# Converting the up and down weights two chunks per transfer, with rows of 8 KB read and 4 KB written, on eight cores of a Trainium2

## The chip, the cores and the metric

The kernel runs on all 8 cores of one Trainium2 chip, one program for all of them. The metric is the device time of the slowest core in microseconds; a run is a median over executions. An integer input called `side` picks one of two instruction streams ("arms"): even cores run arm 0 (the first 2304 frames of a stream), odd cores run arm 1 (the remaining 1792 frames, preceded by a light pass over the first 2304 frames to get the recurrent state).

## The reference

One layer of a hybrid encoder, in float32, for 4 prompt streams of 4096 frames and 32 sample streams of 64 frames, D_MODEL = 1024:

```
h = RMSNorm(x);  [gB | gC | xA | xL | gL] = h @ w_in          # 1024 x 2560
outA = gB * conv3_causal(gC * xA)                             # 512 channels
outB = RG_LRU(conv4_causal(xL) + b) * gelu(gL)                # 512 channels, linear recurrence
x = x + concat([outA, outB]) @ w_out                          # 1024 x 1024
x = x + relu(RMSNorm(x) @ w_up)^2 @ w_down                    # 1024 x 4096, 4096 x 1024
y = RMSNorm(x)
```

The convolution and recurrence states are returned too.

## The kernel before

**Tiles of frames.** Arm 0 has five prompt tiles M0 to M4 of 512, 512, 512, 384 and 384 frames and one sample tile S of 256. Arm 1 has five light tiles L, the tile S and four M tiles. All matmuls are bf16 with float32 sums in PSUM.

**Weights.** w_in, w_up and w_down are cut into 84 chunks of 128 x 1024 numbers: chunks 0 to 19 are w_in, 20 to 51 (from `CH_UP`) w_up, 52 to 83 (from `CH_DOWN`) w_down. They arrive in float32 in `wall`, whose rows are 1024 numbers (4 KB) at a distance of 1040. A DMA issued from GpSimd's queue (queue 0, "software_dynamic") reads float32 and writes bf16, so a row becomes 2 KB. The w_in chunks are converted into SBUF (buffers `ring` and `uT`), used there by tiles S and M0, and copied back to the scratch `wscr` in HBM by SyncE's queue (queue 1). The w_up and w_down chunks are converted from HBM to HBM, `wscr<-wall`: 64 transfers, each 128 rows of 4 KB read and 2 KB written. `wout` goes to SBUF in four conversions whose rows are 8 KB read and 4 KB written.

**The ring.** Each time TensorE needs a chunk, SyncE loads it from `wscr` into one of the ring slots (256 KB, queue 1, 8 rows of 2 KB on each of the 16 DMA engines). Four slots exist until M0's projections are done, then eight; after M0's MLP eight more in `uS`. A load waits for the chunk's conversion (`scr_b[chunk]`) and for TensorE to have left the slot. Inputs x come on ScalarE's queue (queue 10).

**The order of the work.** A planner in Python (`Weaver`) simulates all strands with fixed costs and emits each engine's instructions in the order of the planned start times; on the chip the order is fixed and only semaphores decide times. `g_conv` is the strand of the conversions. Its constants:

```
PACE = {"cv": 6}                 # a conversion is planned no earlier than the landing of the sixth before it
W.CV = 4.4 if chunk < CH_UP else 6.5 if chunk < CH_DOWN else 7.5      # planned us per MB written
MARGIN = 20.0                    # planned us from a conversion's landing to the first load of it
```

and the last number of each DMA request is its size in MB (0.52 for a chunk). The planned landing of a conversion is the previous one's plus size times `CV`. GpSimd's stream holds, in order, these DMA issues, half of the squares of relu (line 535) and small copies; a square that waits holds up the conversions behind it. On the chip a conversion also waits for its semaphore, of which the pool `cv` has 24.

**Lines.** L112 issues all DMAs, L776 and L780 are the input projection (from first-use buffers and from the ring), L989 the output projection, L1037 w_up, L1087 w_down, L697 transposes, L535, L543, L532 helpers of VectorE and ScalarE.

Of the kernel before, what the change touches and what calls it, by code (L numbers as in the profile page):

```python
# [6 lines left out]
F32, BF16 = mybir.dt.float32, mybir.dt.bfloat16  # L7
# [7 lines left out]
CH_UP, CH_DOWN, NCHUNK = 20, 52, 84  # L15
# [3 lines left out]
WPAD = 1040  # L19
# [354 lines left out]
def build_program():  # L374
    nc = bass.Bass("TRN2", target_bir_lowering=False)

    def din(name, shape, dt=F32):
        return nc.dram_tensor(name, list(shape), dt, kind="ExternalInput").ap()

    def dout(name, shape, dt=F32):  # L380
        return nc.dram_tensor(name, list(shape), dt, kind="ExternalOutput").ap()

    xp, xl, xs = din("xp", [NF, D]), din("xl", [128, 8 * NF]), din("xs", [256, D])
    side_d = din("side", [1, 1], mybir.dt.int32)
    wall = din("wall", [NCHUNK, 128, WPAD])
    wout_d = din("wout", [128, 8 * 1024])
    par_d = din("par", [128, PAR_COLS])
    wbd_d = din("wbd", [128, 8 * 128])
    gf_d = din("gf", [D])
    yp, ys = dout("yp", [NF, D]), dout("ys", [256, D])  # L390
    stp_d, sts_d = dout("stp", [128, 24]), dout("sts", [128, 96])
    wscr = nc.dram_tensor("wscr", [NCHUNK, 128, 1024], BF16).ap()

    es = ExitStack()
    tensors, sems = {}, {}
# [11 lines left out]
    def arm(second_half):  # L407
        S = Sched(nc, es, sems)
# [4 lines left out]
        def sb(name, shape, dt=F32):  # L413
            return sbuf(name, shape, dt)

        ring = sb("ring", [128, R * 1024], BF16)
        ring_b = [Buf("ring%d" % i) for i in range(R)]
        slots = [(ring[:, i * 1024:(i + 1) * 1024], ring_b[i]) for i in range(R - 4)]
        wout = sb("wout", [128, 8 * 1024], BF16)
# [74 lines left out]
        ps = psum()  # L494
        bank_b = [Buf("bank%d" % i) for i in range(8)]
        scr_b = [Buf("scr%d" % i) for i in range(NCHUNK)]
        out_events = []

        P_x, P_hb, P_hT, P_T, P_A = Slots(range(8)), Slots(range(2)), Slots(range(NHT)), Slots(range(NT)), Slots(range(1))
        P_x.strict = True  # L500
        P_rs = Slots(range(2))
        P_bank, P_rl, P_stat = Slots(range(8)), Slots(range(3)), Slots(range(5))

        def bank_ap(b, n=512):
            return ps[:, b * 512:b * 512 + n]
# [16 lines left out]
        def PER(dur, mk, rd_, wr_, chunk):  # L522
            def load():
                ap, buf = slots.pop(0)
                slots.append((ap, buf))
                S.dma("sp", ap, wscr[chunk], [scr_b[chunk]], [buf], "ring")
                return ap, buf
            return ("op", "pe", dur, mk, rd_, wr_,
                    {"peek": lambda: (slots[0][1], None), "scr": scr_b[chunk], "load": load})
# [23 lines left out]
        def DMA(q, out, in_, rd_, wr_, pool, mb, **kw):  # L553
            return ("dma", q, out, in_, rd_, wr_, pool, mb, kw)
# [10 lines left out]
        def g_back(oc):  # L565
            ap, bufs = first[oc]
            yield tok(("used", oc))
            yield DMA("sp", wscr[oc], ap, bufs, [scr_b[oc]], "wb", 0.26)

        def g_conv(order):  # L570
            for chunk in order:
                W.CV = 4.4 if chunk < CH_UP else 6.5 if chunk < CH_DOWN else 7.5
                if chunk < CH_UP:
                    ap, bufs = first[chunk]
                    yield DMA("pool", ap, wall[chunk, :, 0:1024], [], bufs, "cv", 0.52)
                    W.spawn(g_back(chunk), 400)
                else:
                    yield DMA("pool", wscr[chunk], wall[chunk, :, 0:1024], [], [scr_b[chunk]], "cv", 0.52)
                if chunk == 15:
                    yield DMA("pool", wbd[:], wbd_d, [], [wbd_b], "par", 0.5)  # L580
                if chunk == 3:
                    for hf in range(4):
                        yield DMA("pool", wout[:, hf * 2048:(hf + 1) * 2048], wout_d[:, hf * 2048:(hf + 1) * 2048], [],
                                  [wout_b[hf]], "cv", 1.05)

        def g_setup():
            yield MSET("pool", identb[:], 0.0, [ident_b])
            yield OP("pool", 0.3, lambda e: e.affine_select(out=identb[:], in_=identb[:], compare_op=ALU.not_equal, fill=1.0,
                                                            base=0, pattern=[[-1, 128]], channel_multiplier=1), [ident_b], [ident_b])
            yield MSET("pool", onesf, 1.0, [ones_b])  # L590
            yield MSET("pool", cst[:, 0:1], 1.0, [cst_b])
            yield MSET("pool", cst[:, 1:2], EPS, [cst_b])
            for t_, bl in ((halx, halx_b), (halp, halp_b), (h0_p, h0_b)):
                yield MSET("pool", t_[:], 0.0, bl)
            W.mark("set0")
# [568 lines left out]
            yield DMA("sp", dst, so[:], [sob], [], "sto", 0.02, allow_slow_non_contiguous=True)  # L1164
            out_events.append(S.last_dma)

        order = [12, 13, 14, 15] + [16, 8, 4, 0, 17, 9, 5, 1, 18, 10, 6, 2, 19, 11, 7, 3] + list(range(CH_UP, NCHUNK))
        W.spawn(g_setup(), -20)
        W.spawn(g_conv(order), 500)
        W.spawn(g_par(), -19)  # L1170
        W.spawn(g_xloads(), -10)
# [19 lines left out]
    with es:  # L1191
        arms = [arm(False), arm(True)]
        emit(nc, [a[0] for a in arms], side_d)
# [59 lines left out]
```

How the kernel before makes its waits and increments, by code:

```python
    def put(e, name, S):  # L149
        for waits, fns, inc in S.prog[name]:
            for k, v in waits:
                e.wait_ge(S.sem[k], v)
            ins = None
            for fn in fns:
                ins = fn(e)
            if inc is not None:
                ins.then_inc(S.sem[inc[0]], inc[1])
```

## Time and profile before

| | us |
|---|---|
| median of 3 runs | 910.05 (909.71 to 910.27) |
| the profiled execution, its own time | 909.05 |
| its span (slowest core, core 6) | 907.5 |
| spans of the 8 cores | 899.8 to 907.5 |
| TensorE busy on core 6 | 839.3 (92%) |
| VectorE, ScalarE, GpSimd busy | 425.2, 376.3, 184.9 |

The 1.55 us between the span and the execution's own time lie outside the instructions. A share of DMA in the profile is the mean share of time in which the 16 DMA engines had a packet; packets under 512 B are the semaphore writes that end a transfer.

### The profile page before, as it was taken

Reading aid. Unit: us, or ns where it says so; the run is one execution under the profiler, and the core shown is the slowest. Engines: PE = TensorE matmul, PEld = TensorE weight load, DVE = VectorE, ACT = ScalarE, POOL = GpSimd, SP = SyncE. Lnnn points to the kernel's source line nnn. Section 1 sums busy time; section 2 is a strip of 40 time slices with the busy share of each in tenths; the row PEclk is TensorE's granted clock in tenths of the full one; section 3 lists DMA queues with packets and bytes.
Section 4 is the critical chain, followed back from the end, with each engine's and each line's share of the span. In section 5 each row is a group of like instructions: output and inputs, shape, how many; then the busy total and the mean of one; then the engine's idle time right before and its main releaser. Section 6 shows DMA issues by size and latency. Waiting matters only on the chain.

```text
span 907.5 us, 15041 instructions; the slowest of 8 cores (899.8 to 907.5 us)
## 1 busy us (share of the span) xinstructions
PE 839.3 (92%) x4392; PEld 428.5 (47%) x4464; DVE 425.2 (47%) x722; ACT 376.3 (41%) x754; POOL 184.9 (20%) x307
## 2 busy tenths in 40 slices
PE   2679789699999999999999999999999899999995
PEld 2444345255564444444444444555445455446542
DVE  4698886663301210636665434575315477514112
ACT  4578738552331000554942134583205485205301
POOL 4132240234453000232100013120003212003200
PEclk9799889899999999999999999999999999999998
DMA  8999999999888534685553369565248852778751
GB/s 237 205 180 215 214 117 130 134 180 177 163 182 168 145 96 126 241 318 172 141 149 84 117 164 300 163 166 161 84 151 254 267 159 73 233 198 271 206 163 73
DMA packets 80441, 158.26 MB, mean 174 GB/s; under 512 B 9184, under 2 KB 9312, under 8 KB 80352
## 3 DMA queue, kind: packets, MB, share of 16 engines
q1 hardware_dynamic: 61632, 111.76, 42.4%
q0 software_dynamic: 15264, 33.30, 23.2%
q10 hardware_dynamic: 3456, 12.14, 4.1%
q8 instruction: 40, 0.66, 0.3%
q14 instruction: 49, 0.40, 0.2%
HBM read 165.75 MB, written 32.57 MB: 219 GB/s over the span
## 4 chain that ended last, share of the span: by engine, by line
PE 82%; DMA 8%; DVE 4%; issue 3%; ACT 2%; POOL 0%; POOLq 0%; DVEq 0%; ACTq 0%; SPq 0%
PE ps L1037 28%; PE ps L1087 27%; PE ps L780 12%; PE ps L989 7%; DMA sb_ring<-wscr 4%; PE ps L776 3%; DMA sb_uT<-wall 3%; PE ps L1079 2%; PE ps L697 1%; PE ps L1097 1%; DMA sb_xsl<-xp 1%; PE ps L855 1%; ACT sb_t_rig L532 1%; PE ps L1074 1%; DVE sb_t_xc L882 1%
## 5 line engine op out<-in xcount | busy, mean ns | idle before, releaser
L1037 PE MATMUL ps<-sb_hT,sb_ring 128*128 128x512 bf16 (+2 forms) x1050 | 194.3, 341 | 6.2 <-DVE sb_a_pb L535 4.3
L532 ACT ACTIVATE sb_junk<-sb_xsl 128x1024 bf16<-128x1024 f32 (+1 forms) x59 | 59.6, 1010 | 269.7 <-DVE sb_xsl L535 256.6
L535 POOL TENSOR_TENSOR sb_uT<-sb_rl 128x512 bf16<-128x512 bf16 (+1 forms) x80 | 83.0, 1038 | 418.4 <-ACT sb_stat L532 272.7
L532 ACT ACTIVATE sb_rl<-ps 128x512 bf16<-128x512 f32 (+2 forms) x192 | 98.1, 525 | 142.2 <-PE ps L1037 127.8
L1037 PEld LDWEIGHTS ps<-sb_hT,sb_ring 128*128 128x128 bf16 x1064 | 104.4, 99 | 91.3 <-issue 8.4
L535 DVE TENSOR_TENSOR sb_xsl<-ps,sb_xsl 128x512 f32<-128x512 f32 (+1 forms) x60 | 46.1, 794 | 200.7 <-PE ps L1087 139.9
L1087 PE MATMUL ps<-sb_ring,sb_uT 128*128 128x512 bf16 x576 | 138.5, 379 | 0.8
L1087 PE MATMUL ps<-sb_uS,sb_uT 128*128 128x512 bf16 x423 | 95.7, 379 | 0.5
L1037 PE MATMUL ps<-sb_hT,sb_uS 128*128 128x512 bf16 (+1 forms) x466 | 92.6, 354 | 0.3
L1087 PEld LDWEIGHTS ps<-sb_ring,sb_uT 128*128 128x128 bf16 x592 | 57.6, 98 | 67.8
L780 PE MATMUL ps<-sb_hT,sb_ring 128*128 128x512 bf16 (+1 forms) x369 | 81.8, 367 | 5.0 <-DMA sb_ring<-wscr 4.6
L535 DVE TENSOR_TENSOR sb_uT<-sb_rl 128x512 bf16<-128x512 bf16 (+1 forms) x80 | 34.0, 425 | 102.6 <-ACT sb_rl L532 90.3
L989 PE MATMUL ps<-sb_wout,sb_mix 128*128 128x512 bf16 x314 | 71.2, 379 | 0.3
L1037 PEld LDWEIGHTS ps<-sb_hT,sb_uS 128*128 128x128 bf16 x472 | 46.0, 98 | 42.9
L1087 PEld LDWEIGHTS ps<-sb_uS,sb_uT 128*128 128x128 bf16 x432 | 42.1, 98 | 49.0 <-issue 0.2
L780 PEld LDWEIGHTS ps<-sb_hT,sb_ring 128*128 128x128 bf16 x376 | 37.1, 99 | 43.4 <-issue 8.4
L532 ACT ACTIVATE sb_t_rig<-sb_t_rig 128x512 f32<-128x512 f32 (+4 forms) x72 | 48.3, 680 | 20.6 <-DVE sb_t_rig L543 19.9
L535 DVE TENSOR_TENSOR sb_hT<-ps,sb_par 128x1024 bf16<-128x1024 bf16 x36 | 43.8, 1220 | 24.7 <-PE ps L697 24.5
L780 PE MATMUL ps<-sb_hT,sb_uS 128*128 128x384 bf16 (+1 forms) x262 | 53.1, 347 | 0.6 <-DVE sb_t_xb L548 0.5
L543 DVE SCALAR_TENSOR_TENSOR sb_t_xc<-sb_t_xb,sb_par,sb_t_xc 128x512 f32<-128x512 f32 (+2 forms) x72 | 46.4, 657 | 13.3 <-ACT sb_t_xc L532 12.1
L532 ACT ACTIVATE sb_t_rig<-sb_t_rig,sb_cst 128x1536 f32<-128x1536 f32 (+5 forms) x48 | 48.2, 1009 | 2.1 <-POOL sb_t_rig L551 0.3
L989 PEld LDWEIGHTS ps<-sb_wout,sb_mix 128*128 128x128 bf16 x320 | 31.2, 98 | 37.5 <-issue 0.7
(100 smaller groups left out, 841.7 us busy)
## 6 DMA issues: line engine op xcount, KB each, us to landing
sb_ring<-wscr SPq DMA_DIRECT2D x240, 256.0 KB, 3.5
sb_uS<-wscr SPq DMA_DIRECT2D x160, 256.0 KB, 3.0
wscr<-wall POOLq DMA_DIRECT2D x64, 256.0 KB, 10.8
sb_xsl<-xp ACTq DMA_DIRECT2D x18, 512.0 KB, 8.7
yp<-sb_xsl POOLq DMA_DIRECT2D x13, 512.0 KB, 7.9
sb_uT<-wall POOLq DMA_DIRECT2D x16, 256.0 KB, 24.1
wscr<-sb_uT SPq DMA_DIRECT2D x16, 256.0 KB, 14.4
sb_wout<-wout POOLq DMA_DIRECT2D x4, 512.0 KB, 13.1
```

The source lines that it names most:

```text
L532: return OP("act", dur, lambda e: e.activation(out=out, in_=in_, func=func, **kw), rd_, wr_)
L535: return OP(eng, dur, lambda e: e.tensor_tensor(out=out, in0=in0, in1=in1, op=op), rd_, wr_)
L543: return OP("dve", dur, lambda e: e.scalar_tensor_tensor(out=out, in0=in0, scalar=scalar, in1=in1, op0=op0, op1=op1), rd_, wr_)
L697: yield PE(0.55, [lambda e, kc=kc: e.transpose(out=pb[:, kc * 128:(kc + 1) * 128], in_=hb_ap[:, kc * 128:(kc + 1) * 128], identity=identb[ ...
L776: lambda e, kc=kc: e.matmul(out=bank_ap(b, N), lhsT=ap[:, kc * 128:(kc + 1) * 128], rhs=h_ap(t, False, kc, col0, N), start=(kc == 0), stop ...
L780: lambda e, kc=kc: e.matmul(out=bank_ap(b, N), lhsT=slot[:, kc * 128:(kc + 1) * 128], rhs=h_ap(t, False, kc, col0, N), start=(kc == 0), st ...
L855: yield PE(0.25, [lambda e, gi=gi, b=b: e.matmul(out=bank_ap(b, N), lhsT=wbd[:, (gi * 4 + c) * 128:(gi * 4 + c + 1) * 128], rhs=T["xcb"][: ...
L882: yield OP("dve", 1.35, lambda e: e.tensor_tensor_scan(out=h, data0=a, data1=i_, initial=h0_p[:, c:c + 1], op0=ALU.mult, op1=ALU.add), [T[ ...
L989: yield PE(4 * 0.217, [lambda e, kc=kc, half=half, b=b, j=j: e.matmul(out=bank_ap(b), lhsT=mix[:, kc * 512 + j * 128:kc * 512 + (j + 1) * ...
L1037: return lambda slot: [lambda e, kc=kc: e.matmul(out=bank_ap(b, q.N), lhsT=slot[:, kc * 128:(kc + 1) * 128], rhs=h_ap(q, True, kc, 0, q.N) ...
L1079: yield PE(32 * 0.217, [lambda e, kc=kc, j=j, bs=bs: e.matmul(out=bank_ap(bs[j]), lhsT=u_ap(t, kc, j * 128, 128), rhs=held[kc // 2][:, (kc ...
L1087: lambda e, i=i, q=q, j=j, b=b: e.matmul(out=bank_ap(b), lhsT=u_ap(q, 2 * kp + i, j * 128, 128), rhs=slot[:, i * 512:(i + 1) * 512], start ...
```

## The change

The 64 conversions of w_up and w_down become 32. The host lays two neighbouring chunks side by side in `wall2`, whose rows are 2048 numbers (8 KB) at a distance of 2064; the scratch `wscr2` has rows of 4 KB that hold a row of both chunks, and a ring load reads its 2 KB half of each row. Both chunks of a pair share one `Buf`, so a load of either waits for the pair's conversion. The planner is told 0.94 MB for a pair instead of twice 0.52; `PACE`, `CV`, `MARGIN` and the 24 semaphores stay, and now count pairs. The w_in chunks and `wout` stay as they are.

```diff
+    wall = din("wall", [CH_UP, 128, WPAD])
+    wall2 = din("wall2", [(NCHUNK - CH_UP) // 2, 128, 2 * 1024 + 16])
...
+    wscr = nc.dram_tensor("wscr", [CH_UP, 128, 1024], BF16).ap()
+    wscr2 = nc.dram_tensor("wscr2", [(NCHUNK - CH_UP) // 2, 128, 2 * 1024], BF16).ap()
...
+        for i in range(CH_UP + 1, NCHUNK, 2):
+            scr_b[i] = scr_b[i - 1]
...
+        def scr_ap(chunk):
+            p, h = divmod(chunk - CH_UP, 2)
+            return wscr[chunk] if chunk < CH_UP else wscr2[p, :, h * 1024:(h + 1) * 1024]
...
-                S.dma("sp", ap, wscr[chunk], [scr_b[chunk]], [buf], "ring")
+                S.dma("sp", ap, scr_ap(chunk), [scr_b[chunk]], [buf], "ring")
...
-                    yield DMA("pool", wscr[chunk], wall[chunk, :, 0:1024], [], [scr_b[chunk]], "cv", 0.52)
+                    p = (chunk - CH_UP) // 2
+                    yield DMA("pool", wscr2[p], wall2[p, :, 0:2048], [], [scr_b[chunk]], "cv", 0.94)
...
-        order = [12, 13, 14, 15] + [16, 8, 4, 0, 17, 9, 5, 1, 18, 10, 6, 2, 19, 11, 7, 3] + list(range(CH_UP, NCHUNK))
+        order = [12, 13, 14, 15] + [16, 8, 4, 0, 17, 9, 5, 1, 18, 10, 6, 2, 19, 11, 7, 3] + list(range(CH_UP, NCHUNK, 2))
```

## Rows read from the trace of the kernel before

**Rows 1.** Spans and mean granted TensorE clock of the cores.

```profile
core 4: 905.1 us, clock 0.980
...
core 6: 907.5 us, clock 0.976
core 7: 902.1 us, clock 0.946
```

**Rows 2.** Core 6 by stretches: length, busy by engine, granted clock, DMA share, GB/s.

```profile
57.00:100.00 43.00, 39.23 (x204) 19.68 (x208) 38.01 (x76) 32.87 (x61) 12.01 (x25) 0.96 1.04 209
100.00:140.00 40.00, 31.43 (x140) 15.37 (x144) 31.20 (x57) 20.64 (x33) 12.47 (x25) 0.83 0.94 147
140.00:180.00 40.00, 31.55 (x170) 15.53 (x172) 26.12 (x42) 29.05 (x50) 7.25 (x12) 0.92 0.99 133
180.00:240.00 60.00, 59.22 (x324) 31.56 (x330) 30.40 (x45) 23.88 (x47) 23.81 (x38) 1.00 0.99 173
240.00:285.00 45.00, 44.74 (x265) 26.23 (x268) 4.70 (x9) 13.96 (x32) 25.77 (x39) 1.00 0.83 163
285.00:700.00 415.00, 412.35 (x2039) 197.50 (x2076) 180.62 (x276) 151.93 (x302) 55.56 (x67) 1.00 0.56 169
```

**Rows 3.** TensorE's waits on core 6: us, times, longest.

```profile
PE ps L780 <- DMA sb_ring<-wscr: 4.6, 1, 4.6
...
PE ps L1037 <- DMA sb_ring<-wscr: 0.7, 2, 0.4
```

**Rows 4.** TensorE in order of time, core 6: start, us, line, count, wait before it.

```profile
119.41 1.04 PE L1037 MATMUL ps<-sb_hT,sb_ring 128*128 128x256 bf16 x8
...
157.56 1.03 PE L1037 MATMUL ps<-sb_hT,sb_ring 128*128 128x256 bf16 x8 [0.34 <-DMA sb_ring<-wscr]
...
161.65 0.61 PE L697 MATMUL ps<-sb_identb,sb_hb 128*128 128x128 bf16 x8 [2.84 <-ACT sb_t_rig L532]
...
176.16 3.57 PE L780 MATMUL ps<-sb_hT,sb_ring 128*128 128x512 bf16 x8 [4.65 <-DMA sb_ring<-wscr]
```

**Rows 5.** Chain that ended last, core 6, around the same place.

```profile
164.07 11.96 DMA sb_ring<-wscr
...
181.93 1.73 PE ps L780 x8
```

**Rows 6.** GpSimd in order of time, core 6: start, us, transfers issued.

```profile
57.42 0.54 POOL L112 DMA_DIRECT2D wscr<-wall  x1
...
130.40 3.64 POOL L112 DMA_DIRECT2D wscr<-wall  x7
157.65 0.56 POOL L112 DMA_DIRECT2D wscr<-wall  x1
```

**Rows 7.** The conversions' issues on core 6: min/median/max ns, first and last start.

```profile
L112 POOL DMA_DIRECT2D wscr<-wall x64: 517/518/1097, 57.4 to 284.0; - x64
```

**Rows 8.** DMA of core 6 from 60 to 66 us, wide rows of `wout`: packets, MB, share.

```profile
DMA packets 278, 1.03 MB, mean 172 GB/s; under 512 B 31, under 2 KB 31, under 8 KB 275
...
q0 software_dynamic: 275, 1.00, 100.1%
```

**Rows 9.** DMA of core 6 from 30 to 40 us, narrow rows into SBUF.

```profile
q0 software_dynamic: 620, 1.13, 72.2%
```

**Rows 10.** DMA of core 6 from 160 to 170 us, narrow rows from HBM to HBM.

```profile
q0 software_dynamic: 475, 0.87, 92.0%
```

**Rows 11.** DMA of core 6 from 180 to 240 us; the last is issues, KB, median us to landing.

```profile
q0 software_dynamic: 2230, 4.05, 59.0%
q1 hardware_dynamic: 3427, 6.23, 39.8%
...
sb_ring<-wscr SPq DMA_DIRECT2D x25, 256.0 KB, 13.1
```

**Rows 12.** DMA of core 7 from 168 to 172 us, both queues with work waiting.

```profile
q0 software_dynamic: 204, 0.37, 79.6%
q1 hardware_dynamic: 205, 0.38, 27.9%
```

More of the change, by code:

```diff
@@ L384, in build_program @@
     side_d = din("side", [1, 1], mybir.dt.int32)
-    wall = din("wall", [NCHUNK, 128, WPAD])
+    wall = din("wall", [CH_UP, 128, WPAD])
+    wall2 = din("wall2", [(NCHUNK - CH_UP) // 2, 128, 2 * 1024 + 16])
     wout_d = din("wout", [128, 8 * 1024])
@@ L391, in build_program @@
     stp_d, sts_d = dout("stp", [128, 24]), dout("sts", [128, 96])
-    wscr = nc.dram_tensor("wscr", [NCHUNK, 128, 1024], BF16).ap()
+    wscr = nc.dram_tensor("wscr", [CH_UP, 128, 1024], BF16).ap()
+    wscr2 = nc.dram_tensor("wscr2", [(NCHUNK - CH_UP) // 2, 128, 2 * 1024], BF16).ap()
     es = ExitStack()
@@ L1215 @@
     shared = {
-        "wall": f(np.pad(wall, ((0, 0), (0, 0), (0, WPAD - 1024)))), "wout": f(f(w_out[0]).reshape(8, 128, 1024).transpose(1, 0, 2).reshape(128, 8192)),
+        "wall": f(np.pad(wall[:CH_UP], ((0, 0), (0, 0), (0, WPAD - 1024)))),
+        "wall2": f(np.pad(wall[CH_UP:].reshape(-1, 2, 128, 1024).transpose(0, 2, 1, 3).reshape(-1, 128, 2048), ((0, 0), (0, 0), (0, 16)))),
+        "wout": f(f(w_out[0]).reshape(8, 128, 1024).transpose(1, 0, 2).reshape(128, 8192)),
         "wbd": f(wbd.reshape(8, 128, 128).transpose(1, 0, 2).reshape(128, 1024)), "gf": f(norm_f_g),
```

## Prediction

> **What bounds the kernel.** I read the cores first: core 6, an even one, sets the time with 907.5 us; the odd core 7 ends 5.4 us earlier, core 4 2.4 us earlier [rows 1]. Then core 6 in stretches [rows 2]. From 180 us on TensorE is busy 59.22 of 60 us and 44.74 of 45 at full granted clock, and 412.35 of 415 after 285 us: there nothing but more waiting can move the end. What could be won lies between 57 us, where the first conversion of an up chunk is issued [rows 7], and 180 us: TensorE is idle 3.8, 8.6 and 8.4 us in the three stretches, 20.8 together, and the clock falls to 0.83 and 0.92. Against that the DMA engines have packets 94 to 104% of the time up to 240 us, so in that stretch they are the scarce thing. Last I asked who makes TensorE wait. Ring loads do in three places for 5.3 us together [rows 3]; the big one is the 4.65 us before 176.16 us [rows 4], and the chain shows why: the load was issued at 164.07 and took 11.96 us [rows 5]. Afterwards eight matmuls took 3.57 us where the same eight take 1.73 us at 181.93: the clock was at its lower level (1.2 instead of 2.4 GHz), another 1.8 us. The other idle time before 180 us has VectorE and ScalarE behind it, as the 2.84 us at 161.65.
>
> **The change, part by part.**
>
> *Fewer issues on GpSimd.* 32 issues of 0.52 us go each [rows 7]: 17 us of GpSimd. It is idle most of every stretch [rows 2], and no wait of TensorE names it: 0 us. If that cover were gone, the squares behind the issues would come 0.5 us earlier each.
>
> *Time of a packet.* Here are the costs that decide. A semaphore packet costs next to nothing, so I divide a queue's share by its data packets, MB over the size. Narrow rows into SBUF: 72.2% of 160 us over 1.13 MB / 2048 B = 552 packets is 209 ns [rows 9]. Wide rows into SBUF: 100.1% of 96 us over 275 - 31 = 244 packets is 394 ns [rows 8]. So doubling a row adds 185 ns, and a byte costs 394 / 418 = 0.94 of before. Narrow rows HBM to HBM cost 286 ns in 180 to 240 us (59.0% of 960 us over 1978 packets [rows 11]) and 346 ns in 160 to 170 (92.0% of 160 over 425 [rows 10]). The wide HBM to HBM packet does not exist before. Its bounds: 394 ns, the SBUF one, and 0.94 x 2 x 286 = 538 ns. I take 286 + 185 = 471 ns, since what HBM adds to a narrow packet looks like waiting, paid once per packet; that is 0.82 of before per byte. The conversions of up and down occupy 64 x 8 x 0.286 = 146 us of the engines before and 32 x 8 x 0.471 = 121 us after (101 to 138): 25 us of engine time is saved between 57 and about 290 us. After 240 us the saving is worth nothing.
>
> The Trainium skill, page "DMA: Bandwidth & Descriptors", section "Anatomy of one DMA", has 2.0 us fixed plus bytes over 436 GB/s for a transfer; by it, if the transfers ran one after another, 32 fewer would save 64 us of queue time. The trace speaks against that sum, not against the rule: in 160 to 170 us queue 0 alone has 92% of the engines, so the fixed part is already overlapped by the transfers behind it.
>
> *What a ring load meets.* In 168 to 172 us on core 7, queue 0 and queue 1 both have work waiting and serve 204 and 205 packets [rows 12]: each engine takes one packet of each in turn. A ring load has 8 packets per engine, of 126 ns (39.8% of 960 us over 3042 [rows 11]). Beside a conversion it is served in 8 x (286 + 126) = 3.3 us now and 8 x (471 + 126) = 4.8 us afterwards (bounds 4.2 and 5.3), and TensorE asks for one every 60 / 25 = 2.4 us from 180 to 240 us [rows 11]. So each load that meets a conversion is at least 1.5 us later, and a stretch with conversions always waiting halves TensorE's supply instead of cutting it by a quarter.
>
> The same skill page, section "Queues, rings and completion order", says the engine "drains a whole packet (≈9-17 descriptors typical, spec ceiling ≤64) from one row's ring before switching". That rule speaks against the change in the same direction: with the 8 rows of a transfer as a turn a load would wait for 8 x 471 instead of 8 x 286 ns, also 1.5 us. The equal counts of the two queues fit either reading.
>
> *When they are issued.* The planner counts six transfers in flight; a pair is 0.94 x 6.5 = 6.1 us of plan, two chunks were 6.8. So the plan runs 6 x 6.1 = 37 us ahead of landings instead of 20, and 10% faster. Before the long wait of GpSimd (27 conversions issued by 134 us in 13 such rows, the last seven in a burst at 130.40, the next at 157.65 [rows 6]) there will be about 27 x 3.38 / 3.06 + 6 = 36 chunks, 18 pairs. In engine time 36 x 0.82 = 29.5 chunks instead of 27: 2.5 x 8 x 0.286 = 5.7 us more work of queue 0 lies ahead of the loads between 130 and 180 us, just where they land as they are needed (the waits of 0.34 and 4.65 us [rows 4]). The last pair is issued some 40 us before the 284.0 us of now. The first pair lands about 3 us later than the first chunk does; its user, S's first up matmuls, comes at 119.41 us [rows 4], over 40 us after: 0 us.
>
> *Ring loads from rows 4 KB apart.* Same packets of 2 KB, 400 loads. Bounds: 0, and a few ns each on 8 packets of a load, hidden from 285 us on, where the share is 0.56 [rows 2]. I take 0.
>
> **The sum for core 6.** Two places where loads are late now, 1.5 us more each: +3.0. The 5.7 us of extra queue 0 work, during which a load comes every 4.8 us and 2.4 are needed: half of it, +2.9. Lower clock behind longer waits, half of the 1.8 us seen: +0.9. Hidden behind the 2.84 us in which TensorE waits for ScalarE at 161.65 anyway: -2.8. Together +4.0. On the profiled execution's own 909.05 that is 913.0; the median of the runs, 910.05, is 1.0 above it, so 914.0.
>
> **Rivals.**
>
> *A. Ring loads are held up by wide packets and earlier conversions: 914.0, own range 911.9 to 921.* For it: equal turns, DMA share 0.99. At the upper packet bound of 538 ns, 36 x 0.94 = 34 chunks are 7 more than 27: 16 us of work, +8 instead of +2.9, and 0.5 us more for each late load: +10.
>
> *B. It cancels or hides: 910.0 (908.2 to 911.9).* With eight slots and 2.4 us per load TensorE has 19 us of cover, and loads land in 13.1; 1.5 us fits in. The 164.07 load meets conversions that are through sooner by 0.82. Then only terms under 2 us remain.
>
> *C. Faster: the saved 25 us of engine time empties queue 0 before the loads of 142 to 170 us come.* Place: the 4.65 us wait and the slow matmuls behind it. Price: 5.3 us of waits and up to 3.3 us at the lower clock (1.8 seen at 176 us, some 1.5 in the matmuls that follow) for core 6, 899; but core 4, 2.4 us shorter, then decides, with smaller waits of the same kind, so about -4.5: 905.5. It decides if the wide packet costs under 27 / 36 x 2 x 286 = 429 ns, for then the earlier issues bring no more engine time than now. 394 ns, the only wide row that the trace has, is below that; 471 is above.
>
> *D. The planner shuffles other work.* The conversions' planned times also enter GpSimd's order. Neither sign is excluded, a few us; it widens the ends and is in the chances below.
>
> The odd cores issue conversions earlier too, and their x loads take turns with wide packets, but they have 5.4 us to lose before they count [rows 1].
>
> **How the numbers follow.** A has 0.49, B 0.24, C 0.27. Within 0.2% (1.8 us) of 910.05 a measurement of this kernel tells nothing; A ends above it, B in it, C below. The range for 8 in 10 takes A's up to 920, all of B, and C down to 906: 906 to 920.
>
> **What would show it.** Right: 32 conversions whose packets are 4 KB at 430 to 540 ns; the last issued near 245 us; ring loads between 130 and 240 us with a median above 14 us; TensorE waits for `sb_ring<-wscr` of 8 us or more on core 6, in the stretches from 140 to 240; no change after 285 us. B: waits for the ring near 5 us. C: these waits near 0 and the granted clock of 140 to 180 above 0.92. The forecast is wrong if the wide packet costs near 394 ns beside other traffic, if the turns are not one packet each for rows of 4 KB, or if TensorE's new waits are for VectorE and ScalarE in a changed order.

## The result, and the profile after

The kernel with the change takes 940.94 us (937.42 to 942.31, 4 runs) against 909.95 us (909.71 to 910.27, 4 runs): a ratio of 1.0338, 95% interval 1.0318 to 1.0357. Some executions of any of these kernels are slower, at a lower granted clock on one half of the chip; the ratios leave them out, the medians in us don't. I had forecast 914.0 with a range of 906 to 920. The side of the answer is right, its size is not: 31 us were lost where I had summed up 4.

The cores of the changed kernel, span and granted clock of TensorE:

```profile
core 4: 932.8 us, clock 0.966
...
core 6: 939.5 us, clock 0.962
core 7: 907.7 us, clock 0.937
```

Against [rows 1] core 6 is 32.0 us longer, core 4 27.7, the odd core 7 only 5.6. So the loss is that of the even cores, and core 6 can be read for it. Its stretches, with the columns of [rows 2]:

```profile
57.00:100.00 43.00, 40.24 (x204) 20.10 (x208) 36.78 (x77) 32.99 (x61) 11.38 (x23) 0.93 1.03 166
100.00:140.00 40.00, 16.99 (x64) 7.14 (x66) 17.31 (x31) 14.57 (x20) 2.44 (x7) 0.70 0.93 197
140.00:180.00 40.00, 32.74 (x177) 17.18 (x178) 28.46 (x48) 23.03 (x41) 7.93 (x14) 0.95 0.94 106
180.00:240.00 60.00, 49.20 (x240) 24.26 (x243) 33.95 (x54) 28.23 (x49) 16.55 (x26) 0.89 0.93 148
240.00:285.00 45.00, 39.98 (x228) 22.16 (x231) 11.95 (x16) 12.12 (x29) 14.01 (x21) 0.96 0.92 160
320.00:700.00 380.00, 376.71 (x1854) 179.22 (x1889) 167.39 (x260) 140.32 (x272) 48.56 (x58) 1.00 0.50 158
```

Up to 100 us TensorE works as before. From 100 to 140 TensorE is busy 16.99 us of 40 instead of 31.43, at a clock of 0.70 instead of 0.83; from 180 to 285 it is idle for 15.8 us of 105, where it had been idle for 1.0. From 320 on it is as full as before. Its waits for loads on core 6, between 57 and 300 us (engine, line, what is waited for: us in total, times, longest):

```profile
PE ps L789 <- DMA sb_ring<-wscr: 24.4, 4, 17.4
PE ps L1046 <- DMA sb_ring<-wscr: 8.5, 4, 3.3
```

L789 and L1046 are L780 and L1037 of before: 32.9 us of waits for the ring where [rows 3] have 5.3. TensorE's order of instructions on the even cores is the same in both kernels, so one instruction can be looked up in both. The first eight matmuls that read a ring load, in TensorE's order of time; before:

```profile
109.05 1.89 PE L780 MATMUL ps<-sb_hT,sb_ring 128*128 128x512 bf16 x8
```

and after:

```profile
128.37 3.47 PE L789 MATMUL ps<-sb_hT,sb_ring 128*128 128x512 bf16 x8 [17.41 <-DMA sb_ring<-wscr]
```

They start 19.3 us later and then take 1.6 us more, at the lower level of the clock: 20.9 us in one place, over half of the whole loss, and at a place that the prediction doesn't name. The chain that ended last shows the rest. After, core 6:

```profile
75.02 20.00 DMA wscr<-sb_uT
95.46 32.77 DMA sb_ring<-wscr
128.37 3.47 PE ps L789 x8
...
164.21 20.08 DMA sb_ring<-wscr
...
193.51 8.64 DMA sb_ring<-wscr
...
205.89 1.73 PE ps L789 x8
...
228.02 22.80 DMA sb_ring<-wscr
...
257.22 5.61 PE ps L998 x26
```

and the two lines of before (its L989 is the L998 of after) that stand beside the last load and the last matmuls:

```profile
206.66 14.85 DMA sb_ring<-wscr
...
224.40 5.61 PE ps L989 x26
```

The matmuls at 181.93 in [rows 5] are those at 205.89 now: 24.0 us late. Those at 224.40 are the ones at 257.22: 32.8 us late, which is all that core 6 loses (32.0). So the loss comes in two lumps, 21 us where the first ring load is used and 9 us between 206 and 257 us, with 3 us net between them and nothing after. Those 3 us lie where the prediction had looked. The matmuls at 156.18, 157.56 and 176.16 us of before, the last two in [rows 4], had waited 0, 0.34 and 4.65 us. Now they start at 179.29, 184.42 and 202.28 us and have waited 2.83, 3.32 and 1.95: 8.1 us instead of 5.0.

```profile
179.29 1.80 PE L1046 MATMUL ps<-sb_hT,sb_ring 128*128 128x256 bf16 x8 [2.83 <-DMA sb_ring<-wscr]
184.42 1.87 PE L1046 MATMUL ps<-sb_hT,sb_ring 128*128 128x256 bf16 x8 [3.32 <-DMA sb_ring<-wscr]
```

What held the first ring load up is on the DMA queues. From 85 to 110 us on core 6 (packets, MB, share of the 16 engines), before:

```profile
q0 software_dynamic: 1106, 2.00, 61.1%
q1 hardware_dynamic: 1780, 3.24, 40.1%
```

and after:

```profile
q0 software_dynamic: 724, 2.64, 85.2%
q1 hardware_dynamic: 726, 1.32, 15.7%
```

After, the two queues move the same number of packets, as if each engine took one of each in turn. 725 packets on 16 engines are 45 turns in 25 us, 0.55 us a turn. A transfer of queue 1 is eight rows and one semaphore packet for each engine, so it takes 9 x 0.55 = 5.0 us. Before, queue 0 ran dry for part of the time, and queue 1 got 1780 packets in the same 25 us. The reason stands in GpSimd's order of time: by 100 us it had issued 13 chunks before, and 10 pairs, 20 chunks, after. And queue 1 has more to do here than I had counted: the copy-backs of the w_in chunks, `wscr<-sb_uT`, stand in it in order ahead of the first ring loads. From 60 to 100 us, issues with KB and median us to landing:

```profile
wscr<-sb_uT SPq DMA_DIRECT2D x8, 256.0 KB, 34.6
sb_ring<-wscr SPq DMA_DIRECT2D x1, 256.0 KB, 32.8
```

Before, 13 copy-backs were issued in that stretch and landed in 15.2 us. The first ring load is delayed twice by this. It reads what a copy-back has written, and in the chain it is issued at 95.46 us, when the copy-back issued at 75.02 has landed; before it went out at 84.01, and landed in 14.5 us:

```profile
84.01 0.44 SPq L112 DMA_DIRECT2D sb_ring<-wscr  x1
```

So it is issued 11.5 us later and takes 18.3 us longer. Of these 29.7 us some 10.5 are covered, since before it had landed at 98.5 us and was needed at 109.05.

### The profile page after: what moved, and what is told of

Read it like the earlier page. It is cut to its first block, busy times and chain, and to the rows that moved or that the text cites. A ratio compares the mean times of both kernels' runs of the same rounds, so it can differ in the third digit from the quotient of the medians.

```text
span 939.5 us, 14946 instructions; the slowest of 8 cores (902.9 to 939.5 us)
## 1 busy us (share of the span) xinstructions
PE 843.6 (90%) x4392; PEld 429.5 (46%) x4464; DVE 423.9 (45%) x722; ACT 375.8 (40%) x754; POOL 169.3 (18%) x275
## 3 DMA queue, kind: packets, MB, share of 16 engines
q0 software_dynamic: 10656, 33.30, 22.6%
## 4 chain that ended last, share of the span: by engine, by line
PE 77%; DMA 16%; issue 3%; DVE 2%; ACT 1%; ACTq 0%; SPq 0%; POOL 0%; DVEq 0%; POOLq 0%
PE ps L1046 27%; PE ps L1096 26%; PE ps L789 12%; DMA sb_ring<-wscr 9%; PE ps L998 6%; DMA sb_uT<-wall 3%; DMA wscr<-sb_uT 2%; DMA sb_xsl<-xp 2%; PE ps L1088 1%; PE ps L706 1%; PE ps L785 1%; PE ps L1106 1%; PE ps L1083 1%; PE ps L864 1%; DVE sb_hb L547 0%
## 5 line engine op out<-in xcount | busy, mean ns | idle before, releaser
L1046 PE MATMUL ps<-sb_hT,sb_ring 128*128 128x512 bf16 (+2 forms) x1050 | 195.3, 342 | 13.5 <-DMA sb_ring<-wscr 8.5
L1046 PEld LDWEIGHTS ps<-sb_hT,sb_ring 128*128 128x128 bf16 x1064 | 104.8, 99 | 99.5 <-issue 15.4
L789 PE MATMUL ps<-sb_hT,sb_ring 128*128 128x512 bf16 (+1 forms) x369 | 84.0, 374 | 24.9 <-DMA sb_ring<-wscr 24.4
L1046 PE MATMUL ps<-sb_hT,sb_uS 128*128 128x512 bf16 (+1 forms) x466 | 92.6, 354 | 0.3
L998 PE MATMUL ps<-sb_wout,sb_mix 128*128 128x512 bf16 x314 | 71.2, 379 | 0.3
L789 PEld LDWEIGHTS ps<-sb_hT,sb_ring 128*128 128x128 bf16 x376 | 37.4, 100 | 65.2 <-issue 31.4
L1046 PEld LDWEIGHTS ps<-sb_hT,sb_uS 128*128 128x128 bf16 x472 | 46.0, 98 | 42.8
L789 PE MATMUL ps<-sb_hT,sb_uS 128*128 128x384 bf16 (+1 forms) x262 | 53.1, 347 | 0.6 <-DVE sb_t_xb L556 0.5
L998 PEld LDWEIGHTS ps<-sb_wout,sb_mix 128*128 128x128 bf16 x320 | 31.3, 98 | 37.3 <-issue 0.2
```

Of the source, the lines that this page charges most:

```text
L789: lambda e, kc=kc: e.matmul(out=bank_ap(b, N), lhsT=slot[:, kc * 128:(kc + 1) * 128], rhs=h_ap(t, False, kc, col0, N), start=(kc == 0), st ...
L998: yield PE(4 * 0.217, [lambda e, kc=kc, half=half, b=b, j=j: e.matmul(out=bank_ap(b), lhsT=mix[:, kc * 512 + j * 128:kc * 512 + (j + 1) * ...
L1046: return lambda slot: [lambda e, kc=kc: e.matmul(out=bank_ap(b, q.N), lhsT=slot[:, kc * 128:(kc + 1) * 128], rhs=h_ap(q, True, kc, 0, q.N) ...
```

## The experiments

All are compared with the kernel before on the same chip, which took 914.74 us beside the first four kernels, 909.91 beside the planned rate, the two halves and "narrow, three ahead", 908.14 beside the fourth and fifth experiments and "wide, three ahead", and 909.49 beside the last two kernels; so the ratios can be compared with each other, the times can't. Beside the ratio stands, as a second measure, the time that TensorE waits for ring loads between 57 and 300 us on cores 0, 2, 4 and 6. It is 4.4, 3.6, 4.5 and 5.3 us before, and 30.2, 33.1, 29.7 and 32.9 after.

**First: which half of the change?** The change makes packets wider, and it also makes the planner issue more conversions earlier. Four kernels separate the two. The first keeps wide transfers but plans each chunk as before (0.52 MB each, both in the order); the even chunk is planned and issues nothing, and the pair is issued at the odd chunk's place and lands both.

```diff
-                    yield DMA("pool", wscr2[p], wall2[p, :, 0:2048], [], [scr_b[chunk]], "cv", 0.94)
+                    if chunk % 2 == 0:
+                        yield DMA("pool", None, None, [], [scr_b[chunk]], "cv", 0.52)
+                    else:
+                        r = DMA("pool", wscr2[p], wall2[p, :, 0:2048], [], [scr_b[chunk]], "cv", 0.52)
+                        W.also[id(r)] = [scr_b[chunk - 1]]
+                        yield r
```

> The 32 wide transfers (8 KB read, 4 KB written per row), but every engine's planned order of before: each pair is issued where the second of its two chunks was, so never more bytes are in queue 0 than before. Theory W (a wide packet doubles the length of a turn, and queue 1, with 8 rows of 2 KB per engine in each copy-back or ring load, gets one packet per turn): the copy-backs and ring loads between 72 and 130 us are slow again; most of the 31 us loss stays, 925 to 938 us; turns near 0.5 us in the stretches where both queues have work. Theory E (the loss comes from conversions issued earlier and further ahead): back to 908 to 913 us.

Measured: 914.54 us, ratio 0.9997 (0.998 to 1.0015). Waits for the ring 7.0, 7.1, 8.8 and 6.5 us. These are 1 to 4 us longer, but wide packets by themselves cost no time that can be measured.

The second has the plan of after (0.94 MB per pair) but two narrow transfers at its place (the lines removed here are those of before):

```diff
-                    yield DMA("pool", wscr[chunk], wall[chunk, :, 0:1024], [], [scr_b[chunk]], "cv", 0.52)
+                    r = DMA("pool", wscr[chunk], wall[chunk, :, 0:1024], [], [scr_b[chunk]], "cv", 0.94)
+                    W.twin[id(r)] = [(wscr[chunk + 1], wall[chunk + 1, :, 0:1024], scr_b[chunk + 1])]
+                    yield r
```

> 64 narrow transfers (4 KB read, 2 KB written per row) in the planned order of the changed kernel: at each place of a pair two narrow transfers are issued. Theory W: the turns are short again (about 0.33 us), so 908 to 916 us, at most some us for the larger amount ahead. Theory E: about the time of the changed kernel, 935 to 942 us.

Measured: 925.3 us, 1.0111 (1.0094 to 1.0128); waits 21.8, 18.8, 19.8 and 17.8. That is between the two expected ranges: the early issues alone cost a third of the loss.

The third issues one transfer per pair whose rows stay 2 KB, 256 of them:

```diff
+                    yield DMA("pool", wscr[chunk:chunk + 2].rearrange("h p c -> p h c"),
+                              wall[chunk:chunk + 2, :, 0:1024].rearrange("h p c -> p h c"), [], [scr_b[chunk]], "cv", 0.94)
```

> 32 transfers of two chunks as in the changed kernel, in its order, but each of the 128 rows is moved as two pieces of 4 KB read and 2 KB written, so packets stay narrow; scratch rows are 2 KB as before. Theory W (the turn is one packet): like the narrow transfers in the new order, 908 to 916 us, with equal packet counts of queues 0 and 1 where both have work. Rival T (the turn is one transfer, so that pairs make it longer whatever their rows are): 930 to 942 us.

Measured: 928.08 us, 1.0144 (1.0124 to 1.0164); waits 20.8, 24.0, 21.0 and 21.0. Half as many transfers with as many rows behave nearly as the second kernel does and not as after: it is the rows that count. Both queues move the same number of packets here too, 1272 and 1275 from 85 to 110 us on core 6, although a transfer of queue 0 now has 16 rows for each engine and one of queue 1 has 8; a turn isn't a transfer.

The fourth is after with three pairs in flight in place of six (`PACE` 3 for chunks from `CH_UP` on):

```diff
+                W.PACE = {"cv": 6 if chunk < CH_UP else 3}
```

> The changed kernel with the planned number of up and down conversions in flight cut from six pairs to three, the same bytes ahead as before; the w_in chunks keep six. Theory W: wide turns remain, but queue 0 runs dry more often while the copy-backs go: 918 to 932 us. Theory E: 908 to 913 us.

Measured: 923.05 us, 1.0092 (1.0067 to 1.0118); waits 24.5, 20.8, 19.3 and 10.4. As many bytes in flight as before, and over two thirds of the loss is gone, but not all. What is left isn't all the ring's. The planner changed TensorE's order of instructions here, which it did not in the three others, and core 6, 1.4 us behind the first kernel at the output projection near 294 us, is 10.2 behind at the end (922.3 and 912.1 us). After 300 us neither waits for a ring load; TensorE is busy longer in all, 852.7 against 844.4 us, with a granted clock of 0.97, 0.93 and 0.97 from 300 to 400, 700 to 800 and 800 to 905 us, where the first kernel has 1.00, 0.95 and 1.00. Why stays open.

The same 25 us of core 6 as above, 85 to 110 us, in the first and the second of these. Wide rows in the order of before:

```profile
q0 software_dynamic: 528, 1.90, 60.7%
q1 hardware_dynamic: 1676, 3.06, 41.0%
```

Narrow rows in the order of after:

```profile
q0 software_dynamic: 1350, 2.46, 73.2%
q1 hardware_dynamic: 1349, 2.46, 29.9%
```

The order decides whether queue 0 is always full: where it is, the counts are equal (1350 and 1349, 724 and 726), and where it isn't, queue 1 has what it needs whatever the rows are (1676 and 1780). The width decides what a turn costs once the counts are equal: queue 1 moves 2.46 MB beside narrow rows and 1.32 MB beside wide ones. That the turns are so short shows in small stretches: with narrow rows in the order of after, none of the 25 stretches of 1 us has the counts of the two queues more than 5 apart, at 54 packets each on 16 engines. If each engine moved nine or more packets of one queue at a time, they would often be more than ten apart (an estimate).

| | rows of 2 KB written | rows of 4 KB |
|---|---|---|
| order of before | 1 | 0.9997 |
| order of after | 1.0111 and 1.0144 | 1.0338 |

Two theories had stood against each other, "width" and "earlier issues". Neither explains the loss alone; earlier issues cost a third of it, and the rest needs the two together.

**Second: is it the planned rate?** After plans 0.94 MB for a pair of twice 0.52. One line, 1.04 instead of 0.94, gives the rate of before with six pairs in flight as in after.

> The changed kernel, but the planner is told 1.04 MB for a pair, as for two chunks before, instead of 0.94; six pairs are still in flight in the plan. Combined theory (queue 0 kept full while the copy-backs go, times the length of a turn): the early issues come from the six pairs ahead, which stay; 925 to 938 us. Rival (the 10% faster planned rate is what keeps the queue full): 912 to 920 us.

Measured: 938.8 us, 1.0306 (1.0284 to 1.0329); waits 30.0, 31.8, 28.7 and 29.6. The rate is worth little, 0.3%; with the fourth kernel above it is the six *pairs* in flight that cost. Three pairs at the old rate were not run.

**Third: which chunks?** Only w_down in pairs, w_up as before, and the reverse, with `W_LO, W_HI = CH_UP, CH_DOWN` (`nar` gives a narrow chunk's place in `wscr`, and the order of the conversions is cut at the same chunks):

```diff
+W_LO, W_HI = CH_DOWN, NCHUNK
...
-        for i in range(CH_UP + 1, NCHUNK, 2):
+        for i in range(W_LO + 1, W_HI, 2):
...
+                elif nar(chunk) is not None:
+                    yield DMA("pool", wscr[nar(chunk)], wall[nar(chunk), :, 0:1024], [], [scr_b[chunk]], "cv", 0.52)
```

> Only the w_down chunks go as wide pairs, planned as in the changed kernel; the w_up chunks are narrow and planned as before. Combined theory: the harm is done by what is in queue 0 between 57 and 130 us, which is as before, so 912 to 919 us with no wait for the first ring load; a later, small harm between 180 and 240 us stays. Rival (the wide packets harm wherever they are): about half of the loss, 925 to 930 us.

> Only the w_up chunks go as wide pairs, planned as in the changed kernel; the w_down chunks are narrow and planned as before. Combined theory: nearly the whole loss, 932 to 942 us, with the wait for the first ring load between 110 and 130 us as in the changed kernel. Rival (harm wherever wide packets are): about half, 925 to 930 us.

Measured: down alone 927.36 us, 1.0184 (1.0165 to 1.0202), waits 17.5, 17.3, 15.4 and 14.3; up alone 925.39 us, 1.0172 (1.0146 to 1.0197), waits 22.6, 21.2, 19.2 and 24.9. Both times my expectation missed and the rival's 925 to 930 us held. By then I held that all of the loss is made early, by the up chunks; it is made in two halves, 1.8% and 1.7%, together about the 3.4% of after. On core 6 the output projection that starts at 224.24 us before starts 14.3 us later in down alone, 18.1 in up alone and 32.8 in after, so here too the two halves add up. The first matmuls on a ring load show where the first half lies, TensorE of core 6 in order of time. Up alone:

```profile
128.93 3.57 PE L795 MATMUL ps<-sb_hT,sb_ring 128*128 128x512 bf16 x8 [22.82 <-DMA sb_ring<-wscr]
```

Down alone:

```profile
107.35 1.89 PE L795 MATMUL ps<-sb_hT,sb_ring 128*128 128x512 bf16 x8
```

Up alone has the first lump, down alone doesn't. Up alone wins 3.5 of its 21.6 us back later, as the 4.65 us wait of before is gone. Down alone loses its time between 190 and 230 us. There, queues of core 4, 191 to 216 us, with the ring loads issued (count, KB, median us to landing); before:

```profile
q0 software_dynamic: 919, 1.67, 53.5%
q1 hardware_dynamic: 1576, 2.87, 48.1%
...
sb_ring<-wscr SPq DMA_DIRECT2D x11, 256.0 KB, 14.4
```

Down alone:

```profile
q0 software_dynamic: 669, 2.47, 79.0%
q1 hardware_dynamic: 659, 1.21, 21.5%
...
sb_ring<-wscr SPq DMA_DIRECT2D x8, 256.0 KB, 30.9
```

Equal counts again, and 659 packets of queue 1 in 25 us are 41 turns per engine: a ring load every 9 / 41 x 25 = 5.5 us, while TensorE asks for one per 2.4 us. In after, where TensorE is late by then, the second lump has its full stretches from 226 to 234 us and again from 242 to 250 (194 and 195 packets), and between them queue 1 is free. Core 6, 226 to 234 us:

```profile
q0 software_dynamic: 171, 0.63, 75.9%
q1 hardware_dynamic: 174, 0.32, 23.8%
```

**Fourth: narrower rows.** If a turn costs what its row costs, rows of 1 KB in the order of after must lose less still. The second kernel again, each row of the conversions cut in two, also of the w_in chunks:

```diff
+    wall = din("wall", [NCHUNK, 128, 2, WPAD // 2])
...
+                    r = DMA("pool", wscr[chunk].rearrange("p (h c) -> p h c", h=2), wall[chunk, :, :, 0:512], [], [scr_b[chunk]], "cv", 0.94)
```

> The narrow transfers in the planned order of the changed kernel (1.1% slower than before), with every row of the conversions, the w_in chunks' too, moved as two pieces of 2 KB read and 1 KB written. Turn theory: when both queues have work, a turn is shorter again, so copy-backs and ring loads pass sooner, ratio to before 1.000 to 1.008, if a packet of half the bytes costs clearly under 172 ns of engine time. Rival (a packet's fixed cost decides; half the bytes save little): conversions get slower, ratio 1.012 to 1.03.

Measured: 910.11 us, 1.0019 (1.0006 to 1.0031), waits 3.0, 4.6, 3.5 and 1.7. Its queues from 85 to 110 us on core 6:

```profile
q0 software_dynamic: 2024, 1.95, 59.1%
q1 hardware_dynamic: 2019, 3.67, 46.8%
```

Equal counts at the third row size, and queue 1 gets 3.67 MB. So with one order, rows of 1, 2 and 4 KB cost 1.0019, 1.0111 and 1.0338. The counts say why: while queue 0 is full, nine turns, a transfer of queue 1, take 1.8, 2.7 and 5.0 us (9 x 16 x 25 us over 2019, 1349 and 726 packets), and TensorE asks for a load every 2.4. It also bounds rival D of the prediction, that the planner's changed order of the other work costs the time: this kernel has that order and loses 0.2%.

**Fifth: the other side of the turn.** Instead of making queue 0's rows narrow I made queue 1's wide: after, with the copy-backs of w_in in pairs too (`win2`, rows of 4 KB), and the same done to before.

```diff
-            yield DMA("sp", wscr[oc], ap, bufs, [scr_b[oc]], "wb", 0.26)
+            yield DMA("sp", win2[oc // 2], t_[:, s_ * 1024:(s_ + 2) * 1024], bufs, [scr_b[oc], scr_b[oc + 1]], "wb", 0.52)
```

> The changed kernel, with the 20 copy-backs of the w_in chunks made as 10 pairs whose rows are 4 KB, so that queue 1 moves twice the bytes in each of its turns while the copy-backs go. Turn theory: the wait for the first ring load near 110 us falls from 17.4 us to 3 to 9 us and the ratio to before from 1.034 to 1.012 to 1.024; the later losses near 160 and 210 us stay. Rival (bandwidth, not turns, holds queue 1 up): no change, 1.03 to 1.036.

> The kernel before with the same ten wide copy-backs. There the first ring load is not waited for, so little is to be won: 0 to 0.4% faster; if the copy-backs' wait for both chunks of a pair delays ring loads instead, up to 0.3% slower.

Measured: on after 930.02 us, 1.0241 (1.022 to 1.0262), waits 24.4, 30.6, 30.1 and 26.0; on before 911.21 us, 1.0032 (1.0017 to 1.0048). Core 6, 85 to 110 us, and the first matmuls on a ring load:

```profile
q0 software_dynamic: 672, 2.46, 76.0%
q1 hardware_dynamic: 670, 2.42, 25.6%
```

```profile
121.49 3.52 PE L793 MATMUL ps<-sb_hT,sb_ring 128*128 128x512 bf16 x8 [10.41 <-DMA sb_ring<-win]
```

Equal counts, and now equal bytes. The wait at the first place goes from 17.41 to 10.41 us, and about 1% of time comes back, although the same edit costs the kernel of before 0.3%. Both are just outside what I expected (3 to 9 us, 1.012 to 1.024), and over all places only cores 0 and 6 wait clearly less. A load now also waits until both chunks of its pair are back, and the order on TensorE changed, so the gain can't be put down to the wide rows alone.

**Last: is there anything to win?** Four kernels look for it, made by edits already shown: before with three in flight; the first experiment with three in flight; and, in the order of before, rows of 1 KB for all chunks or for up and down alone.

> The kernel before with three up and down conversions in flight in the plan instead of six. If a full queue 0 costs the copy-backs and ring loads turns even with narrow rows, this is faster than before: 908 to 913 us where before has 914.7 on the last chip, ring waits of TensorE under 3 us. If six narrow ones ahead are harmless: within 0.2% of before.

> Wide transfers at the places of the second chunk of each pair, in a plan with three chunks in flight instead of six. Turn theory: the least of all kernels ahead in queue 0; ring waits of TensorE under 4 us; 0 to 0.5% faster than before. If the remaining idle time is VectorE's and ScalarE's alone: within 0.2%.

> The kernel before, in its own order, with all 84 weight conversions moved as rows of 2 KB read and 1 KB written. Turn theory, if queue 0 is sometimes full in the old order too (ring waits of 3.6 to 5.3 us on the even cores): ring waits under 3 us and 0.2 to 0.6% faster. If the longer engine time per byte of short rows takes it back at the start, where w_in chunks are waited for: 0.2% slower to 0.3% slower.

> The same, but only for the w_up and w_down chunks; the w_in chunks keep 2 KB rows, so that the start is as before. Turn theory: 0.2 to 0.7% faster. If the old order leaves no backlog that matters: within 0.2%.

| | us | ratio | waits for the ring, cores 0, 2, 4, 6 |
|---|---|---|---|
| narrow, three ahead | 909.07 | 0.9991 (0.9978 to 1.0003) | 6.6, 3.8, 3.3, 6.8 |
| wide, order of before, three ahead | 908.7 | 1.0004 (0.9991 to 1.0017) | 4.5, 6.6, 8.3, 7.0 |
| 1 KB, order of before | 908.44 | 0.999 (0.9979 to 1.0001) | 3.4, 2.3, 3.0, 2.7 |
| 1 KB for up and down | 910.22 | 1.0002 (0.999 to 1.0015) | 2.5, 2.7, 3.7, 2.6 |

None beats the kernel of before by more than the measurement is uncertain. The ring's waits can be brought from about 4.5 to 2.8 us, and no time follows that can be told from none: 1.7 us would be just 0.2%. Three transfers ahead did not shorten the waits, against what I expected (under 3 and under 4 us).

## Why the prediction was right and wrong

**The step that failed: when they are issued.** Its term was "5.7 us more work of queue 0 lies ahead of the loads between 130 and 180 us", half of it, +2.9, and nothing for any load outside that stretch. The count was right: 18 pairs are issued before GpSimd's long wait, as forecast. The places that I named cost about what the sum had for them, 3.1 us more of waits, but by luck: one wait grew from 0.3 to 6.2 us and the other fell from 4.65 to 1.95, where I had 1.5 more for each. And 21 us were lost at 110 us and 9 us between 206 and 257 us, where the sum has nothing. I counted how much work is put in front, as if the loads met it once. What counts is whether queue 0 still runs dry. Six pairs in flight keep it full from 60 to past 110 us, with 20 chunks issued by 100 us instead of 13, and again in bursts later (226 to 234 and 242 to 250 us), and as long as it is full every packet of queue 1 pays a turn. The order of before with the same wide rows costs nothing (0.9997); the order of after costs 1.1 to 1.4% with narrow rows, 3.4% with wide ones.

**A queue I hadn't counted.** I let the loads before 130 us be covered, since no wait there stood in [rows 3]. But queue 1 carries the copy-backs of w_in ahead of them, and these too need eight turns each: landing went from 15.2 to 34.6 us. The first ring load waits for one of them before it is issued, 11.5 us later than before, and then lands 32.8 us after its issue. Up alone shows this lump by itself (22.82 us of wait at the same matmuls, ratio 1.0172), and in the kernel with wide copy-backs it is 7 us smaller. What stays open is how much of the 32.8 us the copy-backs ahead of the load in the queue take; no run took them out of queue 1.

**The time of a packet: 471 ns was too low.** From 180 to 240 us after, with the columns of [rows 11]:

```profile
q0 software_dynamic: 977, 3.54, 54.4%
q1 hardware_dynamic: 2914, 5.30, 37.9%
...
sb_ring<-wscr SPq DMA_DIRECT2D x22, 256.0 KB, 10.9
```

3.54 MB / 4096 B are 864 packets, and 54.4% of 960 us over them is 604 ns. The same way 85 to 110 us give 85.2% of 400 us over 644 packets, 529 ns, and 140 to 180, next, 80.5% of 640 us over 796, 647 ns:

```profile
q0 software_dynamic: 892, 3.26, 80.5%
```

So in after a byte costs as much as in a narrow packet (604 against 2 x 286 = 572), and the saving of 101 ns that I had taken for each is not there. My upper bound, 538, was too low as well. The whole queue shows it, from the page of after, and from that of wide rows in the order of before:

```profile
q0 software_dynamic: 10656, 33.30, 22.6%
```

```profile
q0 software_dynamic: 10656, 33.30, 22.1%
```

22.6% of 939.5 us is 212 us; the page of before has 23.2% of 907.5 us for the same 33.30 MB, 211 us. In the order of before the wide rows take 22.1% of 912.1 us, 202. So of the "25 us of engine time" that I had saved 9 are seen there and none in after, and with them went the ground of rival C (faster below 429 ns). Why the same rows take 10 us more in the order of after stays open. But this term explains little of the loss, as the wide rows cost nothing in the order of before.

**What a ring load meets: the mechanism was right.** "Each engine takes one packet of each in turn" and "8 x (471 + 126) = 4.8 us" against a need of one per 2.4 us: measured 5.0 us from 85 to 110 and 5.5 us from 191 to 216 (down alone). It is called "halves TensorE's supply" in the prediction and then charged with two late loads, +3.0, and half of a backlog. A supply that is halved isn't a term per load: by these numbers TensorE loses about 2.6 us (5.0 - 2.4) for each load it needs after its slots are used up, until queue 0 is dry. That is an estimate; no run counts it load by load.

The Trainium skill, page "DMA: Bandwidth & Descriptors", section "Queues, rings and completion order", has an engine drain a packet of typically 9 to 17 descriptors before it switches rings. The trace agrees that queues take turns, and not with turns of that size, if a packet of the trace is a descriptor: in stretches of 1 us the two counts are never more than 5 apart on 16 engines (second kernel), and a transfer of twice as many rows (third kernel, 1.0144) gets no longer turns (1272 and 1275 packets) and loses about what two transfers lose (1.0111).

The same page's section "Rules for kernel authors" asks to coalesce many small transfers into one large one, and for 1 MiB or more in each for the most bandwidth. Here the number of transfers alone made little difference (1.0111 with 64 of them, 1.0144 with 32), and coalescing two chunks with longer rows cost 3.4%.

**The smaller terms.** The clock: I charged 0.9 us; 1.6 us are seen at the first place alone. "Hidden behind the 2.84 us": of the 2.84 us credited, 0.3 came; TensorE still waits 2.52 us at that place (189.23 us in after), now for VectorE. Fewer issues on GpSimd: 0, right; its busy time falls from 184.9 to 169.3 us, and no time follows. Ring loads from rows 4 KB apart: 0, right by the wide rows in the order of before. "No change after 285 us": right, as 32.8 us are lost by 257 us and 32.0 at the end. The odd cores: they lose 5.6 us on core 7 and still don't count.

**The marks that I gave.** Most of them came true beside a sum that was far off. Ring loads issued between 130 and 240 us land in 14.2 us in the median (12.7 before; "above 14" was the mark), and from 140 to 240 us core 6 waits 10.7 us for them ("8 us or more"). The clock of 140 to 180 us, 0.95, even meets the mark of rival C (above 0.92), because TensorE, 20 us late, does other work there. None of these looks at 110 us. Wrong were the price of a packet and the last pair, which was to be issued near 245 us. The conversions' issues of after, with the columns of [rows 7]:

```profile
L112 POOL DMA_DIRECT2D wscr<-wall x32: 515/550/1105, 57.8 to 290.3; - x32
```

The last is at 290.3, since squares stand between the issues in GpSimd's order and wait for ScalarE, which works on what a late TensorE gives it: the last conversions are earlier in the plan's order and not by the clock. And a median hides a backlog that comes in bursts: that of 180 to 240 us is 10.9 us, below the 13.1 of before, and the loads that count are those of the chain, with 32.77, 20.08 and 22.80 us.

## What to carry to other kernels

Two queues that take turns by row, as these two did, share the engines by the *length of their rows*: before one queue gets longer rows, look at the other one's rows, at how many turns its urgent transfer needs, and at whether the first queue is ever empty. A limit on transfers in flight is a limit on bytes only while the transfers keep their size: whoever doubles the size has to halve the limit, which here gave back over two thirds of a 3.4% loss. And where a cost depends on a queue never running dry, read its length over time, burst by burst, and charge every load in it, the copies ahead of the loads in the same queue too.

## What the runs showed of the hardware

- Queue 0 (GpSimd) and queue 1 (SyncE), both with work, moved the same number of packets, a row or a semaphore write each, for rows of 1, 2 and 4 KB written by queue 0: 2024 and 2019, 1350 and 1349, 724 and 726 packets in 25 us. How many rows a transfer has made no difference to that (1272 and 1275 with twice as many rows in a transfer of queue 0).
- A longer row saved little in conversions from HBM to HBM: 286 ns for 2 KB written, 529 to 647 ns for 4 KB. For all of queue 0's 33.30 MB the engines took 211 us with rows of 2 KB, 202 (order of before) and 212 us (order of after) with 4 KB for up and down, and 224 us (24.7% of 905.0) with 1 KB for all chunks.
- The lower level of the clock, 1.2 instead of 2.4 GHz, after a wait cost nearly the same for waits of 4.65 to 22.82 us: eight matmuls of 128x512 took 3.47 us after 17.41 us of wait, 3.52 after 10.41, 3.57 after 22.82 and 3.57 after the 4.65 in [rows 4], and 1.89 us without one.
